# Loading the first projection behind the modulation, in halves, in a two-block transformer kernel

## The chip, the cores and the metric

The kernel runs on one core of a Trainium2 chip. The metric is the device time of one execution in microseconds (us), taken from the median of several runs. Engines are named as the profile names them: PE is TensorE, DVE is VectorE, ACT is ScalarE, POOL is GpSimd, SP is SyncE, which here does nothing but issue DMAs.

## The reference, cut to what matters

Two transformer blocks run one after the other on x of 256 tokens by 1024 features, all in fp32. The change touches the beginning of the first, the "even" layer:

```python
def even_layer(x, c, norm_g, ada_w, ada_b, in_w, pool_w, pool_scale, sgu_norm_g, sgu_w, sgu_b, out_w):
    h, gate_res = ada_modulate(x, c, norm_g, ada_w, ada_b)   # silu(c) @ ada_w + ada_b -> shift, scale, gate
    a, u, v, gate = _split(h @ in_w, EVEN_SIZES)             # four parts of 1024, 1024, 1024, 2048 columns
    ya = pool_mixer(a, pool_w, pool_scale)                   # window sums, then a 256x256 matmul in each of 4 groups
    yb = spatial_gating(u, v, sgu_norm_g, sgu_w, sgu_b)      # rmsnorm(v), 128x128 matmuls over tokens by head
    y = jnp.concatenate([ya, yb], axis=-1) * jax.nn.silu(gate)
    return x + gate_res * (y @ out_w)

def ada_modulate(x, c, norm_g, ada_w, ada_b):
    ada = jax.nn.silu(c) @ ada_w + ada_b
    shift, scale, gate = jnp.split(ada, 3, axis=-1)
    h = rmsnorm(x, norm_g) * (1.0 + scale[:, None, :]) + shift[:, None, :]
    return h, gate[:, None, :]
```

An "odd" layer with gated linear attention and stick-breaking attention, a final norm and the whole second block follow. The change leaves them as they are.

## The kernel before, in words

All weights stream from HBM in **units** of 1 MB (128 partitions by 2048 floats), 159 of them, in one fixed order. The function `unit` numbers them as the schedule is built, and SP issues them in that order with one loop (L829 to L858), so a wait in front of one unit holds back all that follow. A unit lands in one of three ring places (`raw`, `RAW = 3`), or, early in the program, in memory that is still unused: `EARLY` (L37) maps a unit's number to a place of `work` or `spare` (100 and above), and `REUSED` (L38) names the unit whose semaphore, and in part whose place, it takes over. Before a unit goes into a used place SP waits until what lay there has been consumed (L841 to L856).

There are two sorts of unit. A **projection unit** is a 1024 x 256 slice of a weight matrix. fp32 products are made of three passes: ACT copies the unit to `w_hi` (rounded, L936), DVE subtracts to `w_lo` (L1424), and PE multiplies hi by hi, hi by lo and lo by hi (L2565), 48 matmuls of 128x256 a unit. `w_hi` and `w_lo` have three slots (`SPL = 3`). PE takes a unit when DVE's subtraction is done, and ACT may split into a slot when PE has read its old content. How far ACT and DVE split ahead at a job comes from `split_end` (L777): all units whose slot number is less than three above the job's last one. A **modulation unit** ("ada") is a 512 x 512 slice of `ada_w`. Numbers n = 0, 2, 4, 6 are multiplied on PE (32 matmuls, L2498). All others are multiplied on DVE: four instructions of 128x512 by a column of silu(c) (L1396, L1398), after which PE sums over partitions with four small fp32 matmuls (8 in the records: L2501 up to n = 7, L2495 after that, and there only behind the odd n, since an even n and the next odd n are summed together).

Each engine runs its own in-order program. All are made from one list, `schedule`: the function `run` walks it for each engine, and each engine picks what it knows. DVE handles units strictly in their number's order (`split_next`, L1413): a modulation unit that stands ahead of a projection unit in the list is worked through before that unit is split, even where the schedule names it later.

The start of the schedule before, with unit numbers in brackets:

- `load_x`: PE transposes c and x into features by tokens, ACT copies. Then ada n0 (0), n1 (1), `first_sum` (squares on ACT, sum of squares on PE; behind the squares ACT issues 22 small DMAs of parameter rows, L894 to L920), n2 (2), n3 (3), `first_scale` (DVE: x times rstd), `first_split` (ev 0's weights (4): ACT to w_hi, DVE to w_lo), `params` (PE transposes the parameter rows once all 22 have landed, ACT copies).
- `ada_half` 0 (DVE: scale and shift of the first four feature blocks), n4 (5), n5 (6), `modulate` 0 (h of blocks 0 to 3), n6 (7), n7 (8), `second_split` (ACT), `ada_half` 1, `modulate` 1 (blocks 4 to 7).
- The jobs ev 0 to 3 (4, 9, 11, 13), with ada n8, n9, n10 (10, 12, 14) behind ev 1, 2, 3. Then step `sgu_w` (PE: 8 transposes of 128x128, DVE: two products of 128x512 with the triangle, L1555).
- ea 0 to 3 (15, 17, 19, 21), with n11 to n14 (16, 18, 20, 22) behind each. Then `sgu_v` (ACT: evacuate ea 3, two sums of squares, root; DVE: two scalings, L1560).
- eu 0 to 3 (23 to 26) with the steps `windows` 0 to 3 (DVE: window sums; ACT and DVE split the result), then egb 0 to 3 (27 to 30), each behind a step `sgu_z` (PE: 4 matmuls, DVE: four products of 128x256, L1594, L1597), with the gating of egb's result (ACT silu, DVE product L1989, ACT to y_hi L1360, DVE to y_lo L1991).
- pool 0 to 3 (31), whose banks 0 and 1 ACT evacuates (L1298, L1299) after its last gating copy, then ega 0 (32), which is projected into the bank of pool 0, and so on.

SP issues `sgu_w` and the constants behind `ident` and `ones` ahead of unit 13 (L830), `inv_count` ahead of 24, `sgu_b` ahead of 25.

A job's ACT part in `run` is: split up to `split_end`, then evacuate the job's PSUM bank. There are four banks for the projections (`NBANK = 4`).

## Time and profile before

| | |
|---|---|
| median of 3 runs | 984.38 us (982.93 to 984.91) |
| the profiled execution's own time | 984.94 us |
| its span (first to last instruction) | 983.1 us |
| PE busy in the span | 960.0 us (98%) |
| DVE busy | 649.3 us (66%) |
| ACT busy | 517.9 us (53%) |
| read from HBM | 170.03 MB |

The span is what the trace covers, and some 1.8 us of the execution's own time lie around it. In the timeline a row gives start and length in us, the engine, the line, the operation, what it writes and reads, and how many instructions are merged into it; the bracket gives the engine's idle time just before and what ended it. A letter q behind an engine's name is its issuing sequencer. The records of a matmul of 256 columns are longer (0.28 us) than the step from one to the next.

### The profile page before, as it was taken

The page shows a single profiled execution, that of the slowest core. Times are in us where ns is not written, and L with a number is a line of the kernel's source. Part 1 is how long each engine was busy: PE and PEld are TensorE (multiplying, and loading weights), DVE is VectorE, ACT ScalarE, POOL GpSimd, SP SyncE. Part 2 cuts the span into 40 slices and gives each one's busy share as a digit, 9 for nine tenths or more (in the row PEclk, how much of TensorE's full clock was granted, in tenths as well). Part 3 has the DMA queues.
Part 4 walks back from the last instruction along what each step waited for, and adds up shares of the span by engine and source line. Part 5 has one row for each costly group of instructions (what it writes and reads, how often), then busy time and mean ns, then how long its engine had stood idle before and what let it go on. Part 6 is the DMA issues. An engine that isn't in the chain of part 4 may idle for free.

```text
span 983.1 us, 19802 instructions
## 1 busy us (share of the span) xinstructions
PE 960.0 (98%) x8789; PEld 929.8 (95%) x8789; DVE 649.3 (66%) x751; ACT 517.9 (53%) x604; POOL 1.1 (0%) x12
## 2 busy tenths in 40 slices
PE   7999999999999999999999999999999999999998
PEld 7999999999999999999899999899889999999998
DVE  2997887773766456666699855446676666466565
ACT  3445454456543568853683541377656654354455
POOL 0000000000000000000000000000000000000000
PEclk9999999999999999999999999999999999999998
DMA  9999457855486443485435442224417366556531
GB/s 340 357 370 321 146 167 264 291 177 172 140 289 189 141 142 108 151 254 182 127 92 170 130 130 65 67 86 137 132 44 235 94 207 215 177 181 200 171 109 44
DMA packets 153440, 172.35 MB, mean 175 GB/s; under 512 B 4000, under 2 KB 137692, under 8 KB 153228
## 3 DMA queue, kind: packets, MB, share of 16 engines
q1 hardware_dynamic: 151696, 167.43, 52.7%
q10 hardware_dynamic: 1660, 3.67, 1.1%
q8 instruction: 69, 1.13, 0.5%
q14 instruction: 15, 0.12, 0.0%
HBM read 170.03 MB, written 1.05 MB: 174 GB/s over the span
## 4 chain that ended last, share of the span: by engine, by line
PE 49%; DVE 6%; ACT 3%; issue 1%; DVEq 0%
PE pj L2565 38%; PE m_all L2290 1%; PE m_all L2292 1%; PE m_all L2279 1%; DVE w_lo L1424 1%; PE pj L2524 1%; PE pj L2526 1%; ACT w_hi L936 1%; PE pj L2525 1%; PE pj L2381 1%; PE m_all L2415 1%; PE m_all L2017 0%; DVE work L1836 0%; PE m_all L2442 0%; PE m_all L2320 0%
## 5 line engine op out<-in xcount | busy, mean ns | idle before, releaser
L1424 DVE TENSOR_TENSOR w_lo<-raw,w_hi 128x2048 fp32r<-128x2048 f32 (+1 forms) x126 | 285.4, 2269 | 132.0 <-ACT w_hi L936 131.3
L2565 PE MATMUL pj<-h_hi,w_hi 128*128 128x256 f32 x1224 | 347.4, 284 | 4.0 <-DVE h_lo L1845 1.1
L2565 PE MATMUL pj<-h_hi,w_lo 128*128 128x256 f32 x1224 | 341.8, 279 | 0.0
L2565 PE MATMUL pj<-h_lo,w_hi 128*128 128x256 f32 x1224 | 341.6, 279 | 0.0
L936 ACT ACTIVATE w_hi<-raw 128x2048 fp32r<-128x2048 f32 (+1 forms) x126 | 237.7, 1890 | 85.8 <-PE pj L2565 61.5
L2565 PEld LDWEIGHTS pj<-h_hi,w_hi 128*128 128x128 f32 x1224 | 228.7, 187 | 10.5 <-issue 6.5
L2565 PEld LDWEIGHTS pj<-h_lo,w_hi 128*128 128x128 f32 x1224 | 228.8, 187 | 0.3
L2565 PEld LDWEIGHTS pj<-h_hi,w_lo 128*128 128x128 f32 x1224 | 228.6, 187 | 0.2
L2565 PE MATMUL pj<-y_hi,w_hi 128*128 128x256 f32 x592 | 166.2, 281 | 1.1 <-issue 0.9
L2565 PE MATMUL pj<-y_hi,w_lo 128*128 128x256 f32 x592 | 165.3, 279 | 0.0
L2565 PE MATMUL pj<-y_lo,w_hi 128*128 128x256 f32 x592 | 165.2, 279 | 0.0
L2565 PEld LDWEIGHTS pj<-y_hi,w_hi 128*128 128x128 f32 x592 | 111.3, 188 | 1.8 <-issue 1.2
L2565 PEld LDWEIGHTS pj<-y_lo,w_hi 128*128 128x128 f32 x592 | 111.3, 188 | 0.0
L2565 PEld LDWEIGHTS pj<-y_hi,w_lo 128*128 128x128 f32 x592 | 111.2, 188 | 0.0
L2565 PE MATMUL pj<-w_hi,h_hi 128*128 128x256 f32 x240 | 68.4, 285 | 0.4 <-DVE w_lo L1424 0.4
L2565 PE MATMUL pj<-w_hi,h_lo 128*128 128x256 f32 x240 | 67.4, 281 | 0.0
L2565 PE MATMUL pj<-w_lo,h_hi 128*128 128x256 f32 x240 | 67.4, 281 | 0.0
L1360 ACT ACTIVATE y_hi<-work 128x512 fp32r<-128x512 f32 x32 | 20.3, 633 | 56.3 <-DVE work L1989 31.1
L2565 PEld LDWEIGHTS pj<-w_hi,h_hi 128*128 128x128 f32 x240 | 45.2, 188 | 1.4 <-issue 0.7
L2565 PEld LDWEIGHTS pj<-w_lo,h_hi 128*128 128x128 f32 x240 | 45.2, 188 | 0.0
L2565 PEld LDWEIGHTS pj<-w_hi,h_lo 128*128 128x128 f32 x240 | 45.2, 188 | 0.0
L1295 ACT ACTIVATE work<-pj 128x512 f32<-128x512 f32 x26 | 15.4, 593 | 49.5 <-PE pj L2565 49.5
(401 smaller groups left out, 1204.8 us busy)
## 6 DMA issues: line engine op xcount, KB each, us to landing
raw<-in_odd_in_w_dram SPq DMA_DIRECT2D x28, 1024.0 KB, 5.5
raw<-in_w_in_dram SPq DMA_DIRECT2D x23, 1024.0 KB, 5.3
raw<-in_ada_w_dram SPq DMA_DIRECT2D x22, 1024.0 KB, 6.5
raw<-in_w_ff_in_dram SPq DMA_DIRECT2D x16, 1024.0 KB, 5.4
raw<-in_w_ff_out_dram SPq DMA_DIRECT2D x16, 1024.0 KB, 5.2
raw<-in_even_in_w_dram SPq DMA_DIRECT2D x13, 1024.0 KB, 5.1
raw<-in_even_out_w_dram SPq DMA_DIRECT2D x8, 1024.0 KB, 6.8
raw<-in_odd_out_w_dram SPq DMA_DIRECT2D x8, 1024.0 KB, 5.2
```

The lines of the kernel that those rows point to most:

```text
L936: nc.scalar.activation(w_of(units[u])[0][:, 0:n], raw_of(u)[:, 0:n], ACT.Copy).then_inc(S("split_hi"), 1)
L1295: done_reading(nc.scalar.activation(to, fr, ACT.Copy), key)
L1360: nc.scalar.activation(y_hi[:, c:c + 2, :], gate_tmp("yt", g), ACT.Copy).then_inc(S("y_hi"), 1)
L1424: V.tensor_tensor(lo[:, 0:n], raw_of(u)[:, 0:n], hi[:, 0:n].bitcast(F32), ALU.subtract).then_inc(done, 1)
L2279: m = nc.tensor.matmul(M[2 * c][gs, hcol(h)], at_of(c)[gs, h, :], t_of(c)[gs, h, :], start=True, stop=True)
L2290: nc.tensor.matmul(M[2 * c][gs, hcol(h)], tt_[gs, h, :], um[gs, h, :], start=True, stop=True)
L2292: m = nc.tensor.matmul(M[2 * c + 1][gs, hcol(h)], um[gs, h, :], tt_[gs, h, :], start=True, stop=True)
L2381: last[half] = nc.tensor.matmul(to[:, at * w:(at + 1) * w], src[hs, b, c * P:(c + 1) * P], rhs, start=True, stop=True)
L2415: m = nc.tensor.matmul(M[at // 512][:, at % 512:at % 512 + (i + 1) * P], q_[hs, 2 * g + h // 2, i * P:(i + 1) * P], k_[hs, 2 * g + h // 2, ...
L2524: nc.tensor.matmul(to, wh[:, cs], operand(0, xc), start=(k == 0 and fb == 0), stop=False, skip_group_check=True)
L2525: nc.tensor.matmul(to, wh[:, cs], operand(1, xc), start=False, stop=False, skip_group_check=True)
L2565: m = nc.tensor.matmul(to, a_, b_, start=(s == 0 and q == 0 and (fb == 0 or not together)), stop=(s == len(steps_) - 1 and q == 2), skip_g ...
```

## The change

Units 0 to 7 are now the eight modulation units n0 to n7. Behind them come ev 0's weights in two half units of 512 KB (units 8 and 9: feature blocks 0 to 3 and 4 to 7), then ev 1's in two halves (10 and 11). Each half has a slot of its own, so the slots of all later units move up by two, and the program has 161 units. `EARLY` and `REUSED` give them new places, and a wait for n3's product stands ahead of unit 9.

`first_split` now comes after n7 in the schedule. On ACT it splits units 8, 9 and 10 at once; on DVE it subtracts unit 8, then follow `ada_half` 1, unit 9 (`second_split`) and `modulate` 1. ACT issues the parameter rows in three parts: 4 before silu(c), 11 after it, 7 behind the squares. The wait on `c_turned` and the one on `params_turned` become counts of one semaphore.

No modulation unit stands behind ea 0 any more: n11, n12, n13 stand behind ea 1, 2, 3 (units 19, 21, 23), and n14 stands behind egb 1 (unit 30, ahead of egb 2's unit 31). The step `sgu_w` moves from behind ev 3 to behind eu 1's `windows` step, and its DMA and that of the constants move from ahead of ev 3 to ahead of eu 0 (unit 24). POOL's wait before it clears the padding follows the new places.

```diff
-EARLY = {3: 8, 4: 16, 5: 24, 9: 116, 11: 124, 15: 116, 17: 124, 19: 116, 21: 124}
-REUSED = {9: 3, 11: 4, 15: 9, 17: 11, 19: 15, 21: 17}
+EARLY = {3: 8, 4: 16, 5: 24, 9: 8, 10: 116, 11: 120, 13: 124, 17: 116, 18: 124, 20: 116, 22: 124}
+REUSED = {9: 5, 10: 3, 11: 4, 17: 11, 18: 13, 20: 17, 22: 18}
-ADA_BEHIND = {"ev": (1, 2, 3), "ea": (0, 1, 2, 3), "ega": (1, 3)}
+ADA_BEHIND = {"ev": (1, 2, 3), "ea": (1, 2, 3), "ega": (1, 3)}
+ROW_PARTS = (0, 4, 15, N_ROW_LOADS)
@@ even
-            job(name, kind, i, layout_, [ev0_unit if (name, i) == ("ev", 0) else unit(w, 0, KD, c0 + i * CB, CB)], KD, 0, HR(0))
+            if name == "ev" and i in halved:
+                job(name, kind, i, layout_, halved[i], 4, 0, HR(0))
+            else:
+                job(name, kind, i, layout_, [unit(w, 0, KD, c0 + i * CB, CB)], KD, 0, HR(0))
@@ the schedule
     ada(0, 1, 0, 1)
-    ev0_unit = unit(even_w, 0, KD, 2048, CB)
     step("first_scale")
-    step("first_split")
     step("params")
...
     ada(0, 1, 1, 1)
+    halved = {i: [unit(even_w, 4 * kp, 4, 2048 + i * CB, CB) for kp in range(2)] for i in range(2)}
+    step("first_split")
+    step("ada_half", 1)
     step("second_split")
-    step("ada_half", 1)
     step("modulate", 1)
     even("ev", "copy_t", even_w, 2048, "T")
-    step("sgu_w")
     even("ea", "copy", even_w, 0)
...
         step("windows", i)
+        if i == 1:
+            step("sgu_w")
     for i in range(4):
         step("sgu_z", i)
         job("egb", "gate", i, "F", [unit(even_w, 0, KD, 4096 + i * CB, CB)], KD, 0, HR(0))
+        if i == 1:
+            ada(*later_ada.pop(0))
@@ SP
-                if u == 13:
+                if u == 24:
                     sp.dma_start(cst[:, 2 * P:], consts[:, 2 * P:CONST_AT[1]]).then_inc(S("const_in"), 16)
                     sp.dma_start(w_raw, ins["sgu_w"][0].rearrange("h t s -> t h s")).then_inc(S("sgu_in"), 16)
...
+                if u == 9:
+                    sp.wait_ge(S("ada_acc"), ADA_DVE.index(3) + 1)
@@ ACT
             def load_x():
-                act.wait_ge(S("c_turned"), 1)
+                load_some_rows(0)
+                act.wait_ge(S("rows_turned"), 1)
                 nc.scalar.activation(silu_c[:, :], PJ[0][:, 0:KD], ACT.Silu).then_inc(S("silu_c"), 1)
+                load_some_rows(1)
...
-                squares(0, x, E_["sq"], lambda e, q: e.wait_ge(S("x_ready"), q + 1), load_all_rows)
+                squares(0, x, E_["sq"], lambda e, q: e.wait_ge(S("x_ready"), q + 1), lambda: load_some_rows(2))
             def first_split():
-                split_to(1)
-            def second_split():
-                split_to(2)
+                split_to(3)
@@ DVE
+            def second_split():
+                split_to(2)
```

## Rows read from the trace of the kernel before

**Rows 1.** The page's first part: busy time, share of the span, instructions.
```profile
PE 960.0 (98%) x8789; PEld 929.8 (95%) x8789; DVE 649.3 (66%) x751; ACT 517.9 (53%) x604; POOL 1.1 (0%) x12
```
**Rows 2.** The waits of PE from 20 to 145 us: total, times, longest.
```profile
PE pj L2565 <- ACT work L1299: 0.9, 1, 0.9
PE m_all L2501 <- DVE cst_phase L1398: 0.7, 1, 0.7
PE pj L2017 <- DMA rows<-in_ple_post_norm_dram: 0.6, 1, 0.6
PE pj L2565 <- DVE w_lo L1424: 0.4, 1, 0.4
```
**Rows 3.** The waits of DVE from 88 to 142 us: total, times, longest.
```profile
DVE work L1560 <- ACT small L1030: 3.1, 1, 3.1
DVE y_lo L1991 <- ACT y_hi L1360: 2.8, 4, 0.7
DVE y_lo L1584 <- ACT y_hi L1036: 2.0, 1, 2.0
```
**Rows 4.** Busy time by stretch: length, PE, PEld, DVE, ACT, POOL, clock, DMA share, GB/s.
```profile
50.00:60.00 10.00, 10.00 (x88) 10.00 (x87) 9.05 (x10) 4.76 (x4) 0.00 (x0) 1.00 1.08 368
80.00:90.00 10.00, 10.00 (x89) 10.00 (x88) 4.59 (x2) 6.03 (x8) 0.00 (x0) 1.00 1.03 341
```
**Rows 5.** Timeline of PE from 36 to 69 us.
```profile
37.55 0.36 PE L2565 MATMUL pj<-w_hi,h_hi 128*128 128x256 f32 x1
...
43.82 0.39 PE L2565 MATMUL pj<-w_hi,h_hi 128*128 128x256 f32 x1 [0.35 <-DVE w_lo L1424]
...
61.85 1.04 PE L2017 MATMUL m_all<-cst,work 128*128 128x128 f32 x8
...
68.33 0.95 PE L2495 MATMUL m_all<-cst,cst_phase 128*128 128x1 f32 x8
```
**Rows 6.** Timeline of DVE from 17 to 119 us.
```profile
17.60 1.23 DVE L1443 TENSOR_TENSOR work<-work 128x1024 f32<-128x1024 f32 x1 [2.82 <-ACT work L941]
...
26.51 2.28 DVE L1424 TENSOR_TENSOR w_lo<-work,w_hi 128x2048 fp32r<-128x2048 f32 x1
...
33.88 2.33 DVE L1398 SCALAR_TENSOR_TENSOR cst_phase<-raw,silu_c,cst_phase 128x512 f32<-128x512 f32 x3
...
65.59 1.28 DVE L1555 TENSOR_TENSOR work<-m_all,cst 128x512 f32<-128x512 f32 x2
66.78 0.48 DVE L1396 TENSOR_SCALAR cst_phase<-raw,silu_c 128x512 f32<-128x512 f32 x1
...
69.54 2.28 DVE L1424 TENSOR_TENSOR w_lo<-spare,w_hi 128x2048 fp32r<-128x2048 f32 x1
...
118.83 2.29 DVE L1424 TENSOR_TENSOR w_lo<-raw,w_hi 128x2048 fp32r<-128x2048 f32 x1
```
**Rows 7.** Timeline of ACT from 27 to 142 us.
```profile
27.94 0.38 ACT L967 ACTIVATE cols<-pj 128x256 f32<-128x256 f32 x1 [1.88 <-PE pj L2017]
...
35.45 1.91 ACT L936 ACTIVATE w_hi<-spare 128x2048 fp32r<-128x2048 f32 x1 [2.72 <-DMA spare<-in_even_in_w_dram]
...
83.26 1.92 ACT L936 ACTIVATE w_hi<-raw 128x2048 fp32r<-128x2048 f32 x1 [1.90 <-DMA raw<-in_even_in_w_dram]
87.13 0.60 ACT L1295 ACTIVATE work<-pj 128x512 f32<-128x512 f32 x1 [1.95 <-PE pj L2565]
87.62 1.05 ACT L1027 ACTIVATE work<-work 128x1024 f32<-128x1024 f32 x1
...
141.34 0.56 ACT L1299 ACTIVATE work<-pj,small,cols 128x256 f32<-128x256 f32 x1
```
**Rows 8.** SP's timeline at 36.9 us; then, of the three unit DMAs from 127 to 142 us, the landing.
```profile
36.93 0.37 SPq L857 DMA_DIRECT2D raw<-in_ada_w_dram  x1
...
DMA to landing us min/median/max: 5.0/5.0/5.1
```
**Rows 9.** The chain that ended last: start, length, what.
```profile
410.28 11.31 PE pj L2565 x96
```

More of the change, by code:

```diff
@@ L829, in _ @@
             for u, un in enumerate(units):
-                if u == 13:
+                if u == 24:
                     sp.dma_start(cst[:, 2 * P:], consts[:, 2 * P:CONST_AT[1]]).then_inc(S("const_in"), 16)
                     sp.dma_start(w_raw, ins["sgu_w"][0].rearrange("h t s -> t h s")).then_inc(S("sgu_in"), 16)
-                if u == 24:
+                if u == 25:
                     sp.dma_start(flat(E_["inv"], 4), consts[:, CONST_AT[1]:CONST_AT[2]]).then_inc(S("inv_in"), 16)
-                if u == 25:
+                if u == 28:
                     sp.wait_ge(S("sgu_in"), 16)
                     sp.dma_start(b_all, ins["sgu_b"][0].rearrange("h t -> (h t)").partition_broadcast(P).rearrange("p (h t) -> p h t", h=8)).then_inc(S("sgu_in"), 16)
-                if u == 28:
+                if u == 29:
                     sp.dma_start(cst_phase[:, 0:CONST_PLACES[2][1]], consts[:, CONST_AT[2]:CONST_AT[3]]).then_inc(S("odd_const_in"), 16)
                     sp.dma_start(gate_w, ins["gla_gate_w"][0]).then_inc(S("gate_w_in"), 16)
+                if u == 9:
+                    sp.wait_ge(S("ada_acc"), ADA_DVE.index(3) + 1)
                 if u in REUSED:
@@ L881, in _ @@
             pool.memset(rows[:, :, :], 0.0).then_inc(S("rows_zero"), 1)
-            pool.wait_ge(S("ada_used"), 5)
-            split_done(pool, split_units[0])
+            pool.wait_ge(S("ada_used"), 6)
+            split_done(pool, split_units[1])
             pool.memset(a_pad[:, :, 0:PAD], 0.0).then_inc(S("pad_zero"), 1)
@@ L892, in _, with load_some_rows @@
             act.dma_start(ar(0, 8).rearrange("p (n c) t -> p n (c t)", n=2), x_in).then_inc(S("x_in"), 16)
-            def load_all_rows():
-                act.wait_ge(S("rows_zero"), 1)
+            def load_some_rows(part):
+                if part == 0:
+                    act.wait_ge(S("rows_zero"), 1)
                 n = 0
                 def load_rows(half, r, src):
-                    act.dma_start(rows[r:r + src.shape[0], half, 0:src.shape[1]], src).then_inc(S("rows_loaded"), 16)
+                    nonlocal n
+                    if ROW_PARTS[part] <= n < ROW_PARTS[part + 1]:
+                        act.dma_start(rows[r:r + src.shape[0], half, 0:src.shape[1]], src).then_inc(S("rows_loaded"), 16)
+                    n += 1
                 for half, places in ((0, ROWS_A), (1, ROWS_B)):
@@ L907, in load_all_rows @@
                             load_rows(half, r + 13, a[0:1, 1600:1696])
-                            n += 3
                             continue
@@ L918, in load_all_rows @@
                         load_rows(half, r, a)
-                        n += 1
                 assert n == N_ROW_LOADS, n
@@ L965, in params @@
             def params():
-                act.wait_ge(S("params_turned"), 1)
+                act.wait_ge(S("rows_turned"), 2)
                 nc.scalar.activation(cols[:, :, :], PJ[1][:, 0:2 * P].rearrange("p (c t) -> p c t", c=2), ACT.Copy).then_inc(S("params"), 1)
@@ L1272, in _ @@
                          gn_mean=gn_mean, gn_sq=gn_sq, gn_var=gn_var, at_s=at_s, at_t=at_t, at_o=at_o, mixed=mixed, ffn_pre=ffn_pre,
-                         turn_p=turn_p, split_p=split_p, ple_x=ple_x, ple_post=ple_post, load_x=load_x, first_sum=first_sum, params=params, modulate=modulate, first_split=first_split, second_split=second_split, norm_part=norm_part, norm=norm, final_part=final_part, sgu_v=sgu_v, windows=windows, gla_z=gla_z, gla_decay=gla_decay, gla_kt=gla_kt, gla_o=gla_o, gla_n=gla_n, sb_z=sb_z, sb_c=sb_c, sb_o=sb_o)
+                         turn_p=turn_p, split_p=split_p, ple_x=ple_x, ple_post=ple_post, load_x=load_x, first_sum=first_sum, params=params, modulate=modulate, first_split=first_split, norm_part=norm_part, norm=norm, final_part=final_part, sgu_v=sgu_v, windows=windows, gla_z=gla_z, gla_decay=gla_decay, gla_kt=gla_kt, gla_o=gla_o, gla_n=gla_n, sb_z=sb_z, sb_c=sb_c, sb_o=sb_o)
             def evac(key):
@@ L1906, in _ @@
                          at_s=at_s, mixed=mixed, ffn_pre=ffn_pre, ffn_fold=ffn_fold, ffn_eps=sq_eps, turn_p=turn_p, split_p=split_p, ple_x=ple_x,
-                         ple_post=ple_post, ada_half=ada_half, modulate=modulate, first_sum=first_sum, first_split=first_split, ada_gate=ada_gate, ada_rest=ada_rest, ada_last=ada_last, first_scale=first_scale, norm_part=norm_part, norm=norm, final_part=final_part, final_norm=final_norm, sgu_w=sgu_w, sgu_v=sgu_v, windows=windows, sgu_z=sgu_z, gla_z=gla_z, gla_decay=gla_decay, gla_att=gla_att, gla_n=gla_n, sb_z=sb_z, sb_c=sb_c)
+                         ple_post=ple_post, ada_half=ada_half, modulate=modulate, first_sum=first_sum, first_split=first_split, second_split=second_split, ada_gate=ada_gate, ada_rest=ada_rest, ada_last=ada_last, first_scale=first_scale, norm_part=norm_part, norm=norm, final_part=final_part, final_norm=final_norm, sgu_w=sgu_w, sgu_v=sgu_v, windows=windows, sgu_z=sgu_z, gla_z=gla_z, gla_decay=gla_decay, gla_att=gla_att, gla_n=gla_n, sb_z=sb_z, sb_c=sb_c)
             def evac(key):
@@ L2021, in load_x @@
                 pe.wait_ge(S("c_in"), 16)
-                turn(PJ[0][:, 0:KD], c_rows).then_inc(S("c_turned"), 1)
+                turn(PJ[0][:, 0:KD], c_rows).then_inc(S("rows_turned"), 1)
                 for _ in range(5):
@@ L2044, in params @@
                 turn(PJ[1][:, 0:P], rows[:, 0, :])
-                turn(PJ[1][:, P:2 * P], rows[:, 1, :]).then_inc(S("params_turned"), 1)
+                turn(PJ[1][:, P:2 * P], rows[:, 1, :]).then_inc(S("rows_turned"), 1)
             def first_sum():
```

## The prediction, on record before the changed kernel ran

> **What bounds the kernel now.** I read the page's busy shares first: PE is busy 98% of the span and DVE 66% [rows 1], so the time falls only where PE starts earlier or stops waiting. Next PE's waits in the stretch that the change touches: from 20 to 145 us it waits four times, 2.6 us in all [rows 2]. The first two waits lie in the modulation phase (parameter rows that have not landed, then n5's product on DVE). The third is ahead of ev 1, for DVE's subtraction. The last and longest is ahead of ega 0: its PSUM bank is that of pool 0, and ACT frees it with L1299 at 141.34 + 0.56 = 141.9 us [rows 7].
>
> Then I asked what that last wait hangs on. ACT comes to pool 0 after its copy of egb 3, which waits for DVE. DVE waits three times from 88 to 142 us, always for ACT work that itself waited for DVE (2.8 us in four pieces, 2.0 us), except the first, 3.1 us ahead of L1560 [rows 3]. That one ends a chain on ACT: evacuation of ea 3 at 87.13 us, when PE has finished ea 3, two sums of squares, the root [rows 7]. So from ea 3's end to ega 0's start DVE and ACT are one unbroken chain of 54.8 us (87.13 to 141.9). PE runs beside it with its own 54 us of matmuls and arrives 0.9 us early. In front of the chain DVE has air: from 80 to 90 us it is busy 4.59 us of 10, against 9.05 from 50 to 60 [rows 4]. This decides the change: DVE work taken from ahead of 87 us gains little, DVE work put behind it costs all it takes.
>
> **The head, to ev 0.** (a) ev 0's split leaves its place: 2.28 us of DVE up to 28.79 us [rows 6], right ahead of `ada_half` 0. (b) The rows are issued earlier, so PE's 0.6 us wait for them goes [rows 2]. ACT's copy of the parameters then ends 0.6 us before its 27.94 + 0.38 [rows 7], at 27.75, and `ada_half` 0 starts there, 0.95 earlier than 28.7. n5, h, n6 and n7 follow it, and PE reaches the end of the modulation about 0.9 us earlier: it could start ev 0 at 36.65 instead of 37.55 [rows 5]. n5's product is waited for 0.3 to 0.4 us instead of 0.7.
>
> (c) DVE finishes n7 0.9 earlier than 33.88 + 2.33 [rows 6], at 35.3, and must now subtract unit 8, 1.23 us by the row of 128x1024 [rows 6]: 36.5, hidden behind the rest of PE's n6 and n7. ACT needs about 1.05 us a half [rows 7] and has nothing else to do between blocks 0 to 3, done before DVE begins n7, and block 4, so three fit. Bytes: in the kernel before, the tenth megabyte of weights landed at 35.45 [rows 7]. Now units 8 to 11 end the same ten megabytes, so they land near 31.1, 32.6, 34.0 and 35.5. Enough.
>
> (d) `ada_half` 1 starts when PE ends n7, 36.9. Behind it comes unit 9's subtraction (1.2), only then blocks 4 to 7. Block 4 would be there at 39.85. PE wants it after half a unit; a unit is 11.31 / 2 = 5.65 us [rows 9], so at 39.5: a new stall of 0.4. (e) ev 1 needs only its first half. Before, DVE gave ev 1 free at 43.8 [rows 5]; now 0.9 earlier, plus 1.2 (unit 9), less 1.1 (second half later): 42.95. (f) For ev 2 everything is due: 0.9 earlier, but unit 9 (1.2) and 2 x 1.23 for ev 1 against 2.29 for its whole unit before [rows 6]; in sum 0.4 later than 43.8 + 2.76 (n8) + 2.29 = 48.8, so 49.1 to 49.2. PE comes from ev 1 at 48.7 and waits 0.4. Before, it started ev 2 at 43.82 + 5.8 = 49.6. **PE's gain in the head: 0.5 us**, not 0.9, since DVE is late with ev 2.
>
> **The stream of weights.** Unit 12 (n8) waits for PE to be through with n6: issued at 36.93 before [rows 8], now about 36.0. But the queue is empty from 35.5. A unit issued into an empty queue takes 5.0 us to land [rows 8], against 1.05 MB / 368 GB/s = 2.85 us in a running stream [rows 4]; the stream loses 36.0 + 5.0 - 35.5 - 2.85 = 2.7 us. Against that, 0.83 MB (constants, `sgu_w`) no longer go ahead of ev 3, and n14's megabyte (2.85) no longer ahead of eu 1. Net: ev 3 lands where it did, and so does eu 1, at 83.2 [rows 7]. PE's units up to ea 3 are in time. I cost this at nothing; the cover is n14's absence, and if the gap is longer, eu 1 is late.
>
> **The start of the long chain.** PE ends ea 3 0.5 us earlier from the head. The 8 transposes of `sgu_w` (1.04 as recorded, 0.8 from start to start) have gone to behind eu 1, and n13's four sums (0.95, also 0.8 net) have gone behind ea 3 [rows 5]: 87.1 - 0.5 - 0.8 - 0.8 = 85.0. ACT splits eu 1 first, which lands at 83.2 and takes 1.92: 85.1. The two meet: **the chain starts 2.1 us earlier**, at 85.05. An earlier PE gives nothing more, a later eu 1 costs all of its delay.
>
> **What is put into the chain.** `sgu_w`'s two products on DVE, behind `windows` 1, with nothing to hide them: from 65.59 to the next start at 66.78, 1.2 us [rows 6]. Then n14. The schedule names it behind egb 1, but DVE takes units in order and unit 30 stands ahead of unit 31, egb 2, which `split_end` asks for at job egb 0. So it falls ahead of egb 2's subtraction, at 118.83 before [rows 6]. Price: n12's row, 66.78 to 69.54, 2.8 us [rows 6]. DVE's short waits behind it (0.7 each) are for ACT's copy of what DVE has just made; they can't absorb it. PE has some slack at egb 2, and there the two about meet.
>
> **Sum.** ega 0 starts at 141.9 - 2.1 + 1.2 + 2.8, that is 1.9 us later; PE's wait there grows from 0.9 to about 3. The 0.5 of the head is eaten by it. Behind ega 0 all engines are shifted alike, no unit's order changes and nothing waits for an absolute time. The profiled execution took 984.94 us (983.1 span), so it would be 986.8; the median of the runs, 984.38, is 0.56 below it, and gives **986.2 us**, 0.19% slower. A measurement of this kernel can tell about 0.2% (2 us) from no change, and the forecast stands just on that edge: its own bounds are 985.2 to 987.4 (the pieces of the start each known to some 0.5 us), two fifths of it beyond 986.35.
>
> **A rule on the halves.** Units in a running stream land 2.85 us apart, alone in 5.0 [rows 4, 8], so what a DMA costs beyond its bytes is hidden while another follows. The Trainium skill, "DMA: Bandwidth & Descriptors", section "Rules for kernel authors", asks for at least 1 MiB per DMA, which speaks against the halves. If the extra is not hidden for them, it is a rival of its own: 5.0 - 2.85 = 2.15 us for each of four halves in place of two units, 4.3 more on the stream; eu 1 lands at 87.5, the chain starts 4.3 later, 990.5 us.
>
> **The rivals.**
> 1. *Late start of the chain.* The gap ahead of n8, or the later one ahead of ea 2 (its unit waits for ea 0's subtraction), is longer than worked out, and eu 1 lands 1 to 2 us later. It holds ACT before ea 3's evacuation one for one: 987.7. For it: the meeting at 85.05 has no margin, and before the DMAs ran without a break. Against: n14 is gone from that stretch.
> 2. *Faster: the air of DVE is used.* If DVE or ACT gets ahead in the idle 5.4 us ahead of the chain [rows 4], with eu 2's split done before `sgu_v`, the two insertions (4.0) are covered by it and by the earlier start. It decides once DVE comes to egb 3's gate product less than 0.9 us later than PE needs: then ega 0's wait goes, with the head's gain: 984.4 - 0.5 - 0.9 = 983.0. For it: slots are free and eu 2 is in SBUF by then. Against: ACT's program has `sgu_v` ahead of eu 2's split.
> 3. *It does nothing net.* n14 is not taken where I put it but behind the pool units, or the delay at ega 0 is made good in a later wait: 984.4.
> 4. *The halves pay in full*: 990.5.
>
> **How the numbers follow.** Forecast 0.60, late start 0.17, faster 0.14, nothing net 0.05, halves pay 0.04. Slower by over 0.2%: two fifths of the forecast (0.25), the late start and the halves, 0.46. Within 0.2%: 0.35 + 0.05 = 0.40. Faster: 0.14. The range takes in the late start to 988.2 and reaches down to the faster case, 983.0.
>
> **What would show it.** In the changed kernel's profile: PE's first matmul of ev at 36.6 and a new wait of 0.4 in the middle of ev 0; DVE's w_lo as what ev 2 waits for; n8 landing at 41, with DMA idle ahead of it; ea 3 evacuated at 85; n14's four instructions right ahead of egb 2's subtraction near 118 to 121; PE's wait for L1299's successor near 3 us, ega 0 at 143.8. I am wrong if ega 0 starts before 142, or if PE waits for something else behind it.

## The result, and the profile after

The changed kernel takes **986.84 us** (median of 18 runs, 985.45 to 989.1) beside 984.29 us for the kernel before (18 runs, 982.93 to 985.23): a ratio of 1.003, 95% interval 1.0023 to 1.0036. That is 2.3 to 3.5 us slower. 986.2 was forecast, with 983.0 to 988.2 as range. The profiled execution took 987.8 us, with a span of 986.0.

The page's first part, beside [rows 1], and the waits of PE from 20 to 148 us, beside [rows 2]. The line numbers have moved: L2578 was L2565, L2514 L2501, L1434 L1424, L1309 L1299, L947 L936.

```profile
PE 962.0 (98%) x8789; PEld 932.0 (95%) x8789; DVE 649.6 (66%) x753; ACT 517.8 (53%) x606; POOL 1.5 (0%) x12
```
```profile
PE pj L2578 <- issue: 2.9, 2, 2.2
PE pj L2578 <- ACT work L1309: 1.2, 1, 1.2
PE m_all L2514 <- DVE cst_phase L1408: 0.3, 1, 0.3
PE pj L2578 <- DVE w_lo L1434: 0.2, 1, 0.2
```

The wait for parameter rows is gone, those for DVE's products and for ev's `w_lo` are halved. In their place stand 2.9 us "for issue". PE's timeline shows where these two waits are, and three more points to compare with [rows 5] and with ega 0:

```profile
34.12 0.36 PE L2578 MATMUL pj<-w_hi,h_hi 128*128 128x256 f32 x1
...
46.38 0.38 PE L2578 MATMUL pj<-w_hi,h_hi 128*128 128x256 f32 x1 [0.16 <-DVE w_lo L1434]
...
83.83 0.36 PE L2578 MATMUL pj<-h_hi,w_hi 128*128 128x256 f32 x1 [0.70 <-issue]
...
123.52 0.36 PE L2578 MATMUL pj<-h_hi,w_hi 128*128 128x256 f32 x1 [2.17 <-issue]
144.26 0.39 PE L2578 MATMUL pj<-h_hi,w_hi 128*128 128x256 f32 x1 [1.17 <-ACT work L1309]
```

PE begins ev 0 3.4 us earlier than before (37.55) and ev 2 at 46.38. At 83.83 it waits 0.70 us ahead of eu 0, whose weights had come late (ACT's split of them at 79.49 had waited 5.95 us for the DMA). Then it waits 2.17 us ahead of egb 2 and 1.17 us ahead of ega 0, and starts ega 0 at 144.26, where the kernel before did at 141.96 (its 0.9 us wait in [rows 2] ends there). So 3.4 us won at the head have become 2.3 us lost at ega 0. "Issue" only says that the trace names no releaser; the DVE timeline does. This is DVE, beside [rows 6]:

```profile
32.70 1.22 DVE L1434 TENSOR_TENSOR w_lo<-raw,w_hi 128x1024 fp32r<-128x1024 f32 x1
...
85.65 2.29 DVE L1434 TENSOR_TENSOR w_lo<-raw,w_hi 128x2048 fp32r<-128x2048 f32 x1 [1.92 <-ACT w_hi L947]
89.00 1.42 DVE L1573 TENSOR_SCALAR work<-work,small 128x1024 f32<-128x1024 f32 x2 [1.05 <-ACT small L1040]
...
101.44 1.29 DVE L1568 TENSOR_TENSOR work<-m_all,cst 128x512 f32<-128x512 f32 x2
102.65 2.28 DVE L1434 TENSOR_TENSOR w_lo<-raw,w_hi 128x2048 fp32r<-128x2048 f32 x1
...
118.37 0.49 DVE L1406 TENSOR_SCALAR cst_phase<-raw,silu_c 128x512 f32<-128x512 f32 x1
118.90 2.33 DVE L1408 SCALAR_TENSOR_TENSOR cst_phase<-raw,silu_c,cst_phase 128x512 f32<-128x512 f32 x3
121.14 2.28 DVE L1434 TENSOR_TENSOR w_lo<-raw,w_hi 128x2048 fp32r<-128x2048 f32 x1
```

`sgu_w`'s products take 1.21 us from start to start (101.44 to 102.65), n14 takes 2.77 (118.37 to 121.14), and it stands right ahead of egb 2's subtraction. That one ends at 121.14 + 2.28 = 123.42, and PE starts egb 2 at 123.52: the 2.17 us are a wait for it.

ACT's timeline, beside [rows 7], with the head's halves and the start of the long chain:

```profile
31.35 1.06 ACT L947 ACTIVATE w_hi<-raw 128x1024 fp32r<-128x1024 f32 x1 [2.04 <-DMA raw<-in_even_in_w_dram]
32.85 1.06 ACT L947 ACTIVATE w_hi<-work 128x1024 fp32r<-128x1024 f32 x1 [0.45 <-DMA work<-in_even_in_w_dram]
34.32 1.06 ACT L947 ACTIVATE w_hi<-spare 128x1024 fp32r<-128x1024 f32 x1 [0.41 <-DMA spare<-in_even_in_w_dram]
...
83.70 1.92 ACT L947 ACTIVATE w_hi<-raw 128x2048 fp32r<-128x2048 f32 x1 [1.81 <-DMA raw<-in_even_in_w_dram]
85.53 0.58 ACT L1305 ACTIVATE work<-pj 128x512 f32<-128x512 f32 x1
86.00 1.05 ACT L1037 ACTIVATE work<-work 128x1024 f32<-128x1024 f32 x1
...
143.64 0.56 ACT L1309 ACTIVATE work<-pj,small,cols 128x256 f32<-128x256 f32 x1
```

Look at the reasons in brackets. Before, ACT evacuated ea 3 at 87.13, having waited 1.95 us for PE. Now the evacuation follows eu 1's split without a gap, and that split waited 1.81 us for eu 1's weights. The start of the chain is no longer set by PE, which was through with ea 3 by 82.3 us, but by the stream. The windows show why eu 1 came no earlier (columns as in [rows 4]); the first three lines are the kernel before, the other three the changed one:

```profile
34.00:36.00 2.00, 2.00 (x20) 2.00 (x20) 1.93 (x3) 0.55 (x1) 0.00 (x0) 1.00 1.01 376
58.00:60.00 2.00, 2.00 (x19) 2.00 (x19) 2.00 (x2) 0.03 (x1) 0.00 (x0) 1.00 1.10 353
60.00:62.00 2.00, 2.00 (x20) 2.00 (x19) 1.93 (x3) 0.57 (x1) 0.00 (x0) 1.00 1.05 381
```
```profile
34.00:36.00 2.00, 2.00 (x20) 2.00 (x19) 1.56 (x5) 1.06 (x1) 0.00 (x0) 1.00 0.63 138
58.00:60.00 2.00, 2.00 (x19) 2.00 (x18) 1.11 (x2) 2.00 (x2) 0.00 (x0) 1.00 0.22 71
60.00:62.00 2.00, 2.00 (x19) 2.00 (x19) 2.00 (x2) 0.04 (x1) 0.00 (x0) 1.00 0.92 301
```

There are two holes. The last number of a line is the rate in GB/s; 2 us at the old rate less 2 us at the new one is what the stream missed: (376 - 138) x 2 us = 0.48 MB at 34 us, (353 - 71 + 381 - 301) x 2 us = 0.72 MB at 58 to 62 us. At the rate of [rows 4], 368 GB/s, they are worth 1.3 and 2.0 us. SP's queue shows where both come from:

```profile
33.50 0.37 SPq L866 DMA_DIRECT2D raw<-in_ada_w_dram  x1
...
49.37 2.22 SPq L866 DMA_DIRECT2D raw<-in_ada_w_dram  x1
58.77 0.37 SPq L866 DMA_DIRECT2D spare<-in_even_in_w_dram  x1
```

The first row is n8: SP issues it when PE is through with n6 (its 32 matmuls run from 29.73 to 33.47 us), and until then nothing follows ev 1's halves in the queue. After n11 at 49.37 nothing is issued for nine microseconds, because ea 2's unit takes the place of ea 0's, which DVE has to subtract first. Unit n12, which would not have to wait for that, stands behind ea 2 in the queue; before, it stood ahead of it and was issued at 54.23.

### The profile page after: what moved, and what is told of

Its sections match the earlier page's. It is cut to its first block, busy times and chain, and to the rows that moved or that the text cites. A ratio compares the mean times of both kernels' runs of the same rounds, so it can differ in the third digit from the quotient of the medians.

```text
span 986.0 us, 19810 instructions
## 1 busy us (share of the span) xinstructions
PE 962.0 (98%) x8789; PEld 932.0 (95%) x8789; DVE 649.6 (66%) x753; ACT 517.8 (53%) x606; POOL 1.5 (0%) x12
## 4 chain that ended last, share of the span: by engine, by line
PE 50%; DVE 5%; ACT 3%; issue 1%; DVEq 0%
PE pj L2578 38%; PE m_all L2303 1%; PE m_all L2305 1%; PE m_all L2292 1%; PE pj L2537 1%; ACT w_hi L947 1%; PE pj L2539 1%; PE pj L2538 1%; DVE w_lo L1434 1%; PE pj L2394 1%; PE m_all L2428 1%; PE m_all L2231 1%; PE m_all L2030 0%; DVE work L1849 0%; PE m_all L2455 0%
## 5 line engine op out<-in xcount | busy, mean ns | idle before, releaser
L1434 DVE TENSOR_TENSOR w_lo<-raw,w_hi 128x2048 fp32r<-128x2048 f32 (+2 forms) x127 | 286.5, 2260 | 135.2 <-ACT w_hi L947 134.5
L2578 PE MATMUL pj<-h_hi,w_hi 128*128 128x256 f32 x1224 | 349.3, 285 | 7.3 <-issue 4.1
L2578 PE MATMUL pj<-h_lo,w_hi 128*128 128x256 f32 x1224 | 343.4, 281 | 0.0
L2578 PE MATMUL pj<-h_hi,w_lo 128*128 128x256 f32 x1224 | 342.8, 280 | 0.0
L947 ACT ACTIVATE w_hi<-raw 128x2048 fp32r<-128x2048 f32 (+2 forms) x127 | 238.8, 1883 | 88.5 <-PE pj L2578 60.6
L2578 PEld LDWEIGHTS pj<-h_hi,w_hi 128*128 128x128 f32 x1224 | 230.1, 188 | 14.0 <-issue 9.7
L2578 PEld LDWEIGHTS pj<-h_lo,w_hi 128*128 128x128 f32 x1224 | 230.4, 188 | 0.3
L2578 PEld LDWEIGHTS pj<-h_hi,w_lo 128*128 128x128 f32 x1224 | 230.2, 188 | 0.2
L2578 PE MATMUL pj<-y_hi,w_hi 128*128 128x256 f32 x592 | 166.2, 281 | 1.1 <-issue 0.9
L2578 PE MATMUL pj<-y_lo,w_hi 128*128 128x256 f32 x592 | 165.3, 279 | 0.0
L2578 PE MATMUL pj<-y_hi,w_lo 128*128 128x256 f32 x592 | 165.1, 279 | 0.0
L2578 PEld LDWEIGHTS pj<-y_hi,w_hi 128*128 128x128 f32 x592 | 111.3, 188 | 1.9 <-issue 1.2
L2578 PEld LDWEIGHTS pj<-y_lo,w_hi 128*128 128x128 f32 x592 | 111.3, 188 | 0.0
L2578 PEld LDWEIGHTS pj<-y_hi,w_lo 128*128 128x128 f32 x592 | 111.3, 188 | 0.0
L2578 PE MATMUL pj<-w_hi,h_hi 128*128 128x256 f32 x240 | 68.6, 286 | 0.3 <-DVE w_lo L1434 0.2
L2578 PE MATMUL pj<-w_lo,h_hi 128*128 128x256 f32 x240 | 67.4, 281 | 0.0
L2578 PE MATMUL pj<-w_hi,h_lo 128*128 128x256 f32 x240 | 67.4, 281 | 0.0
L2578 PEld LDWEIGHTS pj<-w_hi,h_hi 128*128 128x128 f32 x240 | 45.2, 188 | 1.6 <-issue 1.0
L2578 PEld LDWEIGHTS pj<-w_lo,h_hi 128*128 128x128 f32 x240 | 45.2, 188 | 0.0
L2578 PEld LDWEIGHTS pj<-w_hi,h_lo 128*128 128x128 f32 x240 | 45.2, 188 | 0.0
```

The source lines that it names most:

```text
L947: nc.scalar.activation(w_of(units[u])[0][:, 0:n], raw_of(u)[:, 0:n], ACT.Copy).then_inc(S("split_hi"), 1)
L1434: V.tensor_tensor(lo[:, 0:n], raw_of(u)[:, 0:n], hi[:, 0:n].bitcast(F32), ALU.subtract).then_inc(done, 1)
L2578: m = nc.tensor.matmul(to, a_, b_, start=(s == 0 and q == 0 and (fb == 0 or not together)), stop=(s == len(steps_) - 1 and q == 2), skip_g ...
```

## The experiments

Each is given against the kernel before as it ran beside it: 983.34 us for the first four kernels, 984.08 for the next four, 984.48 for the last four. All are edits of the changed kernel but the last. The numbers of a view that the verdicts rest on are in the table behind them.

**n14 behind ega 0.** In its place behind egb 1 stands nothing.

```diff
-ADA_BEHIND = {..., "ega": (1, 3)}
+ADA_BEHIND = {..., "ega": (0, 1, 3)}
-        if i == 1:
-            ada(*later_ada.pop(0))
     pool_u = ...
```

> The changed kernel with n14 behind ega 0 instead of egb 1, so that DVE takes it after the long chain. Chain theory: ega 0 starts 2.8 us earlier than in the changed kernel (144.3 to 141.5), some of it given back ahead of ega 1, where DVE has 1.4 us of idle time and 0.5 us of lead for 2.8 us of work: time 984.2 to 985.2, 1.6 to 2.6 below the changed kernel's 986.8. Rival (the loss is from the halves or from the weights' stream, n14 hides in PE's slack at egb 2): 986.8 within 0.5.

Measured: 986.89 us (985.17 to 988.43, 7 runs), ratio 1.0032 (1.0022 to 1.0043). Missed. n14 left the chain as it should, ega 0 started at 142.04 instead of 144.26. But PE then had two new waits, 0.92 us at 168.12 and 1.38 us at 180.94: each ends with DVE's subtraction of that unit (165.74 + 2.29 and 178.56 + 2.28 us), while the changed kernel has one wait of 0.86 us there, at 179.89. That is 1.44 us more of waiting. The rest of what was given back is the clock: behind the wait of 2.55 us ahead of ega 0 it was granted at 0.72 on the mean from 142 to 148 us, which takes 0.28 x 6 = 1.7 us of PE's work, where the changed kernel had 1.00. Together these 3.1 us are more than the 2.2 won at ega 0, and at 181 us PE is 1 us behind the changed kernel. Taking n14 out of the chain is not enough; it needs a place where DVE has air.

**n14 behind ea 3,** as in the kernel before, with n11 to n13 behind ea 0, 1 and 2; the halves and the new place of `sgu_w` stay.

```diff
-"ea": (1, 2, 3)
+"ea": (0, 1, 2, 3)
-        if i == 1:
-            ada(*later_ada.pop(0))
     pool_u = ...
```

> The changed kernel with the modulation units again behind ea 0, 1, 2, 3 (n11 to n14), so that n14 is ahead of the chain on DVE, and its megabyte ahead of eu 1 in the stream. Chain theory: 2.8 us leave the chain; eu 1 lands later by 2.85 less the hole in the stream ahead of ea 2 (about 2.0 us, which closes because n11 is queued there again), so 0.8 later, 84.5: ega 0 at 142.3, time 984.9. If the place of n14 costs nothing: 986.8 or above, since the stream has more ahead of eu 1.

Measured: 983.61 us (983.0 to 986.04, 11 runs), ratio 1.0005 (0.9996 to 1.0014). The slowdown is gone. From eu 1's split to ega 0 it is 2.75 us shorter than in the changed kernel, n14's 2.77. But the run moves four units, and not n14 alone; which of them the time hangs on is seen only beside the run with n11 to n13 a place earlier, below.

**`sgu_w`'s products twice.**

```diff
+link(V.tensor_tensor(w_t[...], M[1 + b][...], bc(K("upto"), 4), ALU.mult))
 V.tensor_tensor(w_t[...], M[1 + b][...], bc(K("upto"), 4), ALU.mult).then_inc(S("sgu_w"), 1)
```

> The changed kernel with sgu_w's two products on DVE made twice (behind eu 1). Chain theory: the chain has no slack, so 1.2 to 1.3 us more on DVE is 1.2 to 1.3 us more at ega 0 and at the end: 988.1. Rival (PE is the bound in this stretch and DVE's work hides): 986.8.

Measured: 987.53 us (986.55 to 989.79, 5 runs), ratio 1.0039 (1.0026 to 1.0052). The interval overlaps that of the changed kernel, so the times alone don't decide between the two forecasts; the profile does. PE's wait ahead of egb 2 grew to 3.43 us and it came to ega 0 without one, at 144.06. The step took 2.66 us on DVE instead of 1.21, and from eu 1's split to ega 0 the profile has those 1.45 us more than the changed kernel's. eu 1 landed 1.65 us earlier in this profile, so ega 0 started no later than in the changed kernel's: the stream's arrival varies more than the term that was tested.

**Whole units for ev 0 and ev 1** in place of the halves.

```diff
-    halved = {i: [unit(...) for kp in range(2)] for i in range(2)}
+    halved = {i: [unit(...) for kp in range(2)] for i in range(0)}
...
-                split_to(3)
+                split_to(2)
...
             def second_split():
-                split_to(2)
+                pass
```

> The changed kernel with ev 0 and ev 1 in whole units behind n7, no halves. Chain theory: PE starts ev 0 some 2.5 to 3 us later (the whole unit lands at 32.8, then 1.9 on ACT and 2.3 on DVE), but eu 1 lands as before and holds the chain's start: no change, 986.8 within 0.6. Rival (the halves are what costs): faster, 984 to 985. Rival (the head sets the end): slower by 2.5, 989.3.

Measured: 987.62 us (987.09 to 989.05, 5 runs), ratio 1.004 (1.0027 to 1.0053), beside 1.003 (1.0023 to 1.0036) with halves. ev 0 starts only at 36.67 us, 2.5 us later than with halves, but eu 1's split starts at 83.42 and ega 0 at 143.97, as in the changed kernel. So when PE starts ev 0 is worth nothing at ega 0; the ratios differ by 0.001, about 1 us, with overlapping intervals. What this run leaves as it is, is the head up to n6: SP issues n8 at 33.50 us in both kernels.

**`sgu_w` ahead of `sgu_v`,** in the changed kernel.

```diff
+    step("sgu_w")
     step("sgu_v")
...
-        if i == 1:
-            step("sgu_w")
```

> The changed kernel with the step sgu_w moved from behind eu 1 to ahead of sgu_v, where DVE waits for the root (its DMA stays ahead of eu 0). Chain theory: 1.2 us leave the chain, ega 0 starts at 143.1 instead of 144.3; the chain's start stays, as eu 1's landing holds it: 1.2 below the changed kernel's 986.8, 985.6. Rival (sgu_w's place costs nothing, the loss is n14's alone): 986.8.

Measured: 985.38 us (983.21 to 987.94, 11 runs), ratio 1.001 (1.0 to 1.002). As expected: the products' 1.2 us leave the chain (59.37 us from eu 1's split to ega 0, against 60.56). ega 0 starts 3.1 us earlier in this profile; the other 1.9 us are an earlier eu 1.

**The same with n14 behind ea 3.** Both insertions are out of the chain.

> n14_back (983.6, ega 0 at 141.4 in its trace, with 2.5 us of wait ahead of it and then 3.4 us at half clock) with sgu_w ahead of sgu_v too. Chain theory: ega 0 at 140.2. The wait ahead of it falls to 1.3; if the fall of the clock comes from the long wait, it stays away and gives back another 1.7: 980.7 to 982.4. If the clock's fall is not tied to the wait: 982.4.

Measured: 984.03 us (981.72 to 987.41, 11 runs), ratio 0.9998 (0.9986 to 1.0009). Missed, by 1.6 us or more. The chain is as short as expected, 56.59 us, but eu 1's split began at 84.60 us, not at 83.59 as with n14 behind ea 3 alone, and ega 0 at 141.19. The wait ahead of it was 1.73 us, and the clock did not fall.

**Five dummy matmuls ahead of ega 0,** with n14 behind ea 3: PE is kept at work in the wait.

```diff
+    step("keep_busy", "ega")
     even("ega", "gate", even_w, 3072)
```

> n14_back with five dummy matmuls of 256 columns (fp32, about 2 us) on PE ahead of ega 0, where it waits 2.5 us; they add nothing to the output. If the wait is what lowers the clock to half for 3.4 us behind it (141.6 to 145.0 in n14_back's trace), the fall is gone and the time is 1.7 us below n14_back, 981.9. Rival (the fall has another cause, or ega 0 is held by more than its bank): 983.6 or a little above.

Measured: 985.35 us (983.09 to 987.83, 12 runs), ratio 1.0009 (0.9998 to 1.002). The time missed the 981.9. The clock did what was expected: PE was through with the pool at 141.63 us and could start ega 0 only at 144.38. The dummies filled this from 141.63 to 143.95, 0.42 us of waiting were left, and no lower clock followed (1.00 from 141 to 148 us). Without them the wait would have been near 2.7 us. Since two of nine such waits had no fall either (below), one profile doesn't prove that the dummies kept it away. The time shows nothing of it (ratio 1.0009 beside 1.0005 with n14 behind ea 3), and in this profile eu 1 came 3 us later than there.

**Another order of units:** both insertions out, ev 2's unit ahead of n8's and n14 behind eu 0, to close the hole at 34 us.

```diff
-"ev": (1, 2, 3), "ea": (1, 2, 3)
+"ev": (2, 3), "ea": (0, 1, 2, 3)
...
+        if i == 0:
+            ada(*later_ada.pop(0))
         step("windows", i)
```

> sgu_mid with ev 2's unit ahead of n8 (n8 to n13 behind ev 2, ev 3, ea 0 to 3, n14 behind eu 0), so that the queue is not empty while SP waits for PE to be through with n6. Stream theory: the hole of 1.3 us at 34 to 36 closes, eu 1 lands 1.3 earlier and so does the chain's start: ega 0 at 138.9, where PE arrives by itself, no long wait, no fall of the clock: 978 to 980. Rival (the order of units is worth nothing, PE sets the start): as sgu_mid.

Measured: 983.7 us (982.68 to 985.42, 11 runs), ratio 0.9995 (0.9986 to 1.0005). Missed. The hole at 34 us closed (347 GB/s from 34 to 36 us), but it moved: SP now stood behind DVE's product for n8 until 47.72 us, and eu 1's split started at 83.80. The time is that of both out (984.03), as the rival had it.

**n11 to n13 behind ea 0 to 2,** in the changed kernel; n14 stays behind egb 1.

```diff
-"ea": (1, 2, 3)
+"ea": (0, 1, 2)
```

> The changed kernel with modulation units 11, 12 and 13 behind ea 0, 1 and 2 instead of ea 1, 2 and 3. If the hole in the weight stream at 58 to 60 us is what made eu 1's weights late, it closes, eu 1's weights land some 2 us earlier (81.7 us), the chain on VectorE and ScalarE from there to ega 0 begins as early as TensorE's end of ea 3 lets it (83.2 to 83.6 us), ega 0 starts at about 142.3 us instead of 144.3, and the time is about 985.0 us. If the stream doesn't set the time, it stays at 986.8 us.

Measured: 985.0 us (983.67 to 987.58, 11 runs), ratio 1.0008 (0.9998 to 1.0018). As expected. The second hole is closed (351 GB/s from 60 to 62 us), eu 1's split starts 3.1 us earlier, ega 0 3.0 us earlier. Not all of it is the hole's: n8 had been issued 1.2 us earlier already (32.30 us for 33.50). From there to eu 1's landing it is 48.25 us for 50.18, so the hole is worth 1.9 us in this pair. The ratios (1.0008 and 1.003) say 2.2.

The run also gives the only clean test of n14's place, since n14 behind ea 3 differs from it by n14 alone: 0.52 and 0.27 us above the kernel before, with overlapping intervals. The chain is 2.87 us longer with n14 behind egb 1 (60.68 and 57.81), but without n14's megabyte ahead of it eu 1 starts 3.0 us earlier (80.57 and 83.59), and ega 0 comes at the same time, 141.25 and 141.40. So the 2.8 us that n14 puts into the chain are real, and its place in the stream pays for them; what made the changed kernel slow beside this one is the hole.

**`sgu_v` behind ea 2** in the changed kernel: ACT's squares and root and DVE's scalings come a unit earlier.

```diff
+            if (name, i) == ("ea", 2):
+                step("sgu_v")
             if i in ADA_BEHIND[name]:
...
-    step("sgu_v")
```

> The changed kernel with the step sgu_v (squares, root and scaling of v) behind ea 2 instead of behind ea 3. If the time is set by the chain on VectorE from eu 1's weights to ega 0's, this takes 2.4 to 2.5 us out of it: from the landing of eu 1's weights to ega 0's first product 58.1 us instead of 60.6, and about 984.4 us. If only the late landing of eu 1's weights or the lower clock sets it, 986.8 us as the changed kernel.

Measured: 984.9 us (982.7 to 987.62, 11 runs), ratio 1.0003 (0.9993 to 1.0013). Near the chain theory's 984.4, and far from the rival's 986.8. The weights of eu 1 land as late as in the changed kernel (83.77 us), and ega 0 starts 1.9 us earlier all the same. 2.9 us went out of the chain behind the split, and 1.0 came back ahead of it, since ACT now does the squares and the root before it turns to eu 1 (84.67).

**All three: n14 behind ea 3, `sgu_w` ahead, `sgu_v` behind ea 2.**

> The changed kernel with modulation unit 14 as in the kernel before, the sgu weights' step ahead of sgu_v and sgu_v behind ea 2. By the chain theory the landing of eu 1's weights to ega 0 is 54.1 us instead of 56.6, so that ega 0 starts at 138 to 139 us, where TensorE comes by itself: no long wait there, no lower clock behind one, 979.5 to 981.5 us. If what is taken out of this chain is waited for behind ega 0 in any case, 983 to 984 us.

Measured: 983.75 us (980.92 to 985.35, 12 runs), ratio 0.9988 (0.9977 to 0.9998). Missed by over 2 us; the number is the rival's, but not its mechanism, since behind ega 0 no wait grew (0.76 us at 176.31, 0.87 in the kernel before). The chain behind the split is the shortest of all, 54.84 us, but eu 1 landed at 84.87 and its split, behind ACT's squares, began at 85.83, so ega 0 started at 140.67.

**The kernel before, with `sgu_v` behind ea 2.**

> The kernel before with sgu_v behind ea 2. The chain theory: VectorE's chain is 2.5 to 2.8 us shorter, and TensorE, which waits 0.9 us at ega 0, no longer waits: 0.9 us less than the kernel before, 983.2 to 983.5 us beside 984.1. If the chain on VectorE doesn't set ega 0's start in that kernel, no change.

Measured: **981.92 us** (981.07 to 982.94, 8 runs), ratio 0.9974 (0.9964 to 0.9984): faster than both kernels, and by more than the 0.9 us expected. The waits of PE from 60 to 185 us are a single one, and ACT frees pool 0's bank at 138.68 + 0.56 = 139.24 us, where the kernel before did at 141.9:

```profile
PE pj L2566 <- issue: 0.3, 1, 0.3
```
```profile
138.68 0.56 ACT L1300 ACTIVATE work<-pj,small,cols 128x256 f32<-128x256 f32 x1
```

Besides the 0.9 us at ega 0, another wait shrank with it, that of 0.87 us at 177.60, to 0.27 at 174.93: 1.5 us together. In the profile PE was also some 0.9 us earlier already at the end of ea 3, where the edit had not yet reached it, as it had been at ev 0 (36.63 us for 37.55). Whether the rest of the 2.6 us is the edit's or the head's scatter stays open.

**What the fourteen kernels show together.** us into the profile; the fourth column is the third less the second.

| kernel | eu 1's split starts on ACT | ega 0 starts on PE | from split to ega 0 | PE's waits at egb 2, ega 0 | clock at 0.5 right behind |
|---|---|---|---|---|---|
| before | 83.26 | 141.96 | 58.70 | 0, 0.89 | no |
| changed | 83.70 | 144.26 | 60.56 | 2.17, 1.17 | yes (egb 2) |
| whole units | 83.42 | 143.97 | 60.55 | 1.06, 2.58 | yes |
| n11 to n13 earlier | 80.57 | 141.25 | 60.68 | 0.80, 2.58 | no |
| products twice | 82.05 | 144.06 | 62.01 | 3.43, 0 | yes (egb 2) |
| `sgu_w` ahead | 81.82 | 141.19 | 59.37 | 1.04, 2.58 | no |
| n14 behind ea 3 | 83.59 | 141.40 | 57.81 | 0, 2.49 | yes |
| n14 behind ega 0 | 84.23 | 142.04 | 57.81 | 0, 2.55 | yes |
| dummy matmuls | 86.58 | 144.38 | 57.80 | 0, 0.42 | no |
| both out | 84.60 | 141.19 | 56.59 | 0, 1.73 | no |
| other order | 83.80 | 140.40 | 56.60 | 0, 2.58 | yes |
| `sgu_v` early | 84.67 | 142.36 | 57.69 | 0.38, 2.53 | yes |
| all three | 85.83 | 140.67 | 54.84 | 0, 1.23 | no |
| before, `sgu_v` early | 83.36 | 140.00 | 56.64 | 0, 0 | no |

The rows behind three of these lines, first n14 behind ea 3, then n11 to n13 earlier, then `sgu_v` early; of each, from ACT's and PE's timelines:

```profile
83.59 1.92 ACT L945 ACTIVATE w_hi<-raw 128x2048 fp32r<-128x2048 f32 x1 [1.83 <-DMA raw<-in_even_in_w_dram]
...
141.40 0.46 PE L2576 MATMUL pj<-h_hi,w_hi 128*128 128x256 f32 x1 [2.49 <-ACT work L1307]
```
```profile
80.57 1.92 ACT L947 ACTIVATE w_hi<-raw 128x2048 fp32r<-128x2048 f32 x1 [1.91 <-DMA raw<-in_even_in_w_dram]
...
141.25 0.39 PE L2578 MATMUL pj<-h_hi,w_hi 128*128 128x256 f32 x1 [2.58 <-ACT work L1309]
```
```profile
84.67 1.91 ACT L948 ACTIVATE w_hi<-raw 128x2048 fp32r<-128x2048 f32 x1
...
142.36 0.58 PE L2579 MATMUL pj<-h_hi,w_hi 128*128 128x256 f32 x1 [2.53 <-ACT work L1310]
```

In the fourth column the two insertions add up to a tenth. 56.6 us is the chain with neither; `sgu_w`'s products add 1.2, n14 2.8, the doubled products some 1.4 more. `sgu_v` behind ea 2 does not add up so well: it takes off 2.9 in the one kernel and 1.75 in the other. The kernel before stands out with 58.7: there ACT still waited for PE ahead of ea 3's evacuation, 1.95 us, and that wait is inside the stretch. In the last line PE comes to ega 0 by itself, 0.8 us after its bank is free, so that line is PE's.

The start varies from 80.6 to 86.6 us, also between kernels that are alike up to there. Most of that is decided in the head, before n8 is issued. Where the order of units up to eu 1 is the same, the time from n8's issue on SP to eu 1's landing is nearly the same too:

| units up to eu 1 | profiles | n8 issued at | from there to eu 1's landing |
|---|---|---|---|
| as in the changed kernel | changed, whole units, products twice, `sgu_w` ahead, n14 behind ega 0, `sgu_v` early | 31.91 to 34.25 | 49.8 to 50.2 |
| n11 to n13 earlier | n11 to n13 earlier | 32.30 | 48.25 |
| n11 to n14 earlier | n14 behind ea 3, dummy matmuls, both out, all three | 33.04 to 35.88 | 50.5 to 51.2 |

So the time at ega 0 has three parts: when PE is through with n6, which varies by 4 us from profile to profile for reasons not found; the stream from there, by the order of units; and the chain, by the schedule.

## Why the prediction was right

**What bounds the kernel** was read rightly: PE arrives at ega 0 by itself only a little early, and the chain on DVE and ACT ends later as soon as anything is put into it. The whole-units run is the plainest evidence: PE starts ev 0 2.5 us later, and nothing of it is seen at ega 0.

**The insertions** were priced at 1.2 and 2.8 and measured at 1.21 and 2.77. n14 was placed rightly ahead of egb 2's subtraction, in unit order and not where the list has it. The rivals that the kernel would do nothing net, or get faster because DVE's air covers the insertions, have fallen by the time. But that n14 costs its 2.8 us net is not so: beside n11 to n13 earlier its place makes no difference, since its megabyte no longer stands ahead of eu 1. The prediction had both terms, the one under the stream and the other under the chain.

**The head** failed as a term. 36.65 was forecast for ev 0 and 34.12 came. Of the 3.4 us, 0.9 was reasoned. What else there is shows in part on PE's and ACT's timelines, first of the kernel before, then of the changed one:

```profile
20.55 1.89 PE L2050 MATMUL m_all<-work,cst 128*128 128x256 f32 x8
22.98 0.32 ACTq L899 DMA_DIRECT2D rows<-in_ple_post_norm_dram  x1
23.34 0.47 ACT L949 ACTIVATE rstd<-m_all,small 128x256 f32<-128x256 f32 x1 [5.77 <-PE m_all L2050]
```
```profile
18.25 1.89 PE L2063 MATMUL m_all<-work,cst 128*128 128x256 f32 x8
20.18 0.47 ACT L960 ACTIVATE rstd<-m_all,small 128x256 f32<-128x256 f32 x1 [3.84 <-PE m_all L2063]
```

Before, the last of the 22 row DMAs was issued right ahead of the root that x's scaling waits for; each takes ACT's queue some 0.3 us. PE's sum, which the root needs, was done at 22.44, and the root came at 23.34: the issues held it up by 0.9 us. With 15 of them ahead of the squares it follows the sum at once. The prediction looked at when the rows land, not at what their issue holds up on ACT. The other 2.3 us of the root's 3.2 are PE's: it came to the sum that much earlier, 1.2 of it because x was there earlier (it waited 0.72 us for x, 1.92 before), 1.1 because the eight matmuls between x and n0 took 1.95 us, not 3.02. Why is not settled. The stall of 0.4 in ev 0 did not come, and that at ev 2 was 0.16. In the eleven profiles with this head and the halves ev 0 started between 33.6 and 36.5 us, 34.3 on the mean, in the two with the old head at 37.55 and 36.63. So most of the 3.4 is the change's, and 0.9 was too little.

**The stream** was 0.5 us late (83.7 for 83.2), and that it was no more is luck. n8 was forecast to be issued at 36.0 and was at 33.50, 2.5 us earlier, since PE was through with n6 that much earlier. From there to eu 1 the forecast has 47.2 us, and it took 50.2. Two errors of 2.5 and 3.0 us went against each other. With n8 at 36.0 the regularity of the second table above puts eu 1 near 86, and the long chain's start 2.3 us later than it was (an estimate from 36.0 + 50.0). The gap at n8 was forecast as 2.7 us and measured as 1.3. The hole ahead of ea 2 was named only in a rival and left at nothing in the sum; it measured 2.0. A smaller first hole fits an n8 that went out earlier than forecast. Since PE was through with ea 3 by 82.3 us, eu 1's weights alone set the chain's start. (A slip of reading on the way, without effect: the unit issued at 36.93 in the kernel before is n9, n8 had gone at 32.14. It is the one that waits for PE's n6 there, so the time was the right one.)

**The start of the chain** came out at 85.53 instead of 85.05, and DVE's scaling of v at 89.00 against 90.63, 1.63 us earlier where 2.1 had been forecast. **The sum** was then 141.96 - 1.63 + 1.21 + 2.77 = 144.3, against 144.26 in the trace and 143.8 forecast. PE's idle time was forecast as 3 us at ega 0. It was 2.17 + 1.17, the greater part at egb 2: "the two about meet" was wrong by these 2.17 us. PE had more time to spare than that shows: behind the wait at egb 2 its clock was granted at 0.72 on the mean from 124 to 130 us, which took 0.28 x 6 = 1.7 us of its work, and it still had to wait at ega 0. With so much to spare the head's extra gain went into waiting:

```profile
124.00:130.00 6.00, 6.00 (x40) 6.00 (x40) 5.16 (x8) 2.92 (x3) 0.00 (x0) 0.72 0.85 289
```

**The halves** land 1.50 and 1.47 us apart (ACT's splits at 31.35, 32.85 and 34.32 each wait for their DMA), half of the 2.85 us of a whole unit in [rows 4]. So in a running stream the cost of a DMA beyond its bytes was hidden for 512 KB as well. The Trainium skill, "DMA: Bandwidth & Descriptors", section "Rules for kernel authors", asks for at least 1 MiB per DMA; here the measurement decides: no cost of the half size was seen, in the landings or in the time beside whole units.

**Behind ega 0** the median lost 2.55 us (2.3 to 3.5 by the ratio) where ega 0 lost 2.30, and the span 2.9. The prediction had all engines shifted alike. For the profile's extra 0.6 us there is a cause in the clock, below; what the median's 0.25 is, within its interval, is not settled.
